# Zero-block products in TensorE's waits, earlier clearing of the dense sums and 96-row rotations in a two-block transformer kernel

## What is computed

```python
for l in range(2):                                  # first block
    h = rmsnorm(x, norm1_g[l]) * (1 + sc1) + sh1
    x = x + g1 * token_mix(h, ...)                  # w_in, recurrence, attention, w_out
    h = rmsnorm(x, norm2_g[l]) * (1 + sc2) + sh2
    x = x + g2 * grouped_moe(h, w_router, ...)      # top 2 of 16 experts
x = rmsnorm(x, final_g)
for layer in range(2):                              # second block
    y = recurrent_mixer(hn, ...) if layer == 0 else chunk_attention(hn, ...)
    h = h + g1 * y
    h = h + g2 * (square(relu(hn2 @ w1)) @ w2)      # dense MLP
```

## Time and profile before

| | us |
|---|---|
| median of 3 runs (2007.92 to 2010.44) | 2008.97 |
| the profiled execution | 2012.4 |
| its span | 2010.8 |
| PE busy in it | 1846.0 (92%) |

### The profile page before, as it was taken

One profiled execution on the slowest core, in us unless ns is written; L12 is line 12 of the kernel. 1 busy time (PEld: TensorE's weight loads), 2 busy tenths in 40 slices (PEclk: granted clock), 3 DMA queues, 4 the chain that ended last, 5 costly groups with the idle time before them and its releaser, 6 DMA issues.

```text
span 2010.8 us, 26693 instructions
## 1 busy us (share of the span) xinstructions
PE 1846.0 (92%) x11077; PEld 1309.6 (65%) x11080; DVE 675.8 (34%) x1189; ACT 591.5 (29%) x988; POOL 66.9 (3%) x136
## 2 busy tenths in 40 slices
PE   4999996989995999997999995999899999898998
PEld 2888685323333888684333334766699988588998
DVE  4583413000003583513000004313355551516554
ACT  2335311111113325311111112141254423525443
POOL 0000001100001000001101000000000000000000
PEclk8999997999997999997999997999899999998999
DMA  9669653999976665753999947879944553133540
GB/s 391 256 265 394 269 241 120 421 428 427 428 308 232 252 256 226 299 228 145 427 428 427 412 173 282 340 312 428 384 185 167 182 194 120 69 126 129 195 178 21
DMA packets 52732, 541.04 MB, mean 269 GB/s; under 512 B 6817, under 2 KB 11169, under 8 KB 21665
## 3 DMA queue, kind: packets, MB, share of 16 engines
q1 hardware_dynamic: 42656, 505.66, 62.4%
q0 software_dynamic: 9984, 34.09, 4.6%
HBM read 589.53 MB, written 29.62 MB: 308 GB/s over the span
## 4 chain that ended last, share of the span: by engine, by line
PE 82%; DMA 8%; DVE 6%; ACT 2%; DVEq 1%; issue 1%; SPq 0%; POOL 0%; POOLq 0%; ACTq 0%; PEldq 0%
PE bank L933 15%; PE bank L1230 14%; PE bank L896 9%; PE bank L897 9%; PE bank L898 9%; PE bank L1254 6%; DMA ring<-in_w_up 5%; PE bank L943 3%; PE bank L1060 1%; PE bank L1338 1%; PE bank L1426 1%; DMA ring<-in_ada 1%; PE bank L1359 1%; DMA ring<-in_lru_w_out 1%; PE bank L1208 1%
## 5 line engine op out<-in xcount | busy, mean ns | idle before, releaser
L896 PE MATMUL bank<-split_x,split_w 128*128 128x256 f32 x1024 | 292.3, 285 | 1.1 <-DVE split_w L2401 1.1
L897 PE MATMUL bank<-split_x,split_w 128*128 128x256 f32 x1024 | 291.9, 285 | 0.0
L898 PE MATMUL bank<-split_x,split_w 128*128 128x256 f32 x1024 | 291.8, 285 | 0.0
L896 PEld LDWEIGHTS bank<-split_x,split_w 128*128 128x128 f32 x1024 | 198.9, 194 | 2.9 <-DVE split_w L2401 2.9
L897 PEld LDWEIGHTS bank<-split_x,split_w 128*128 128x128 f32 x1024 | 198.9, 194 | 0.0
L898 PEld LDWEIGHTS bank<-split_x,split_w 128*128 128x128 f32 x1024 | 198.8, 194 | 0.0
L2283 DVE TENSOR_TENSOR hidden<-cqkv,bank 128x256 f32<-128x256 f32 x46 | 19.4, 421 | 523.7 <-ACT cqkv L1681 523.7
L2401 DVE TENSOR_TENSOR split_w<-ring,split_w 128x1024 fp32r<-128x1024 f32 x128 | 156.3, 1225 | 94.7 <-ACT split_w L1794 94.7
L933 PE MATMUL bank<-h_t,ring 128*128 128x256 f32 x736 | 164.5, 385 | 11.9 <-DVE h_t L2084 8.1
L933 PEld LDWEIGHTS bank<-h_t,ring 128*128 128x128 f32 x736 | 141.2, 193 | 35.9 <-DVE h_t L2084 9.3
L1794 ACT ACTIVATE split_w<-ring 128x1024 fp32r<-128x1024 f32 x128 | 133.8, 1049 | 94.4 <-PE bank L898 91.4
(11 more groups left out here) (351 smaller groups left out, 2322.9 us busy)
## 6 DMA issues: line engine op xcount, KB each, us to landing
ring<-in_ada SPq DMA_DIRECT2D x48, 2048.0 KB, 12.2
ring<-in_w_down SPq DMA_DIRECT2D x32, 2048.0 KB, 16.6
ring<-in_w_gate SPq DMA_DIRECT2D x32, 2048.0 KB, 13.1
ring<-in_w_up SPq DMA_DIRECT2D x32, 2048.0 KB, 18.3
ring<-in_mlp_w SPq DMA_DIRECT2D x32, 2048.0 KB, 7.7
ring<-in_w_in SPq DMA_DIRECT2D x16, 2048.0 KB, 11.9
mix<-in_w_gate SPq DMA_DIRECT2D x14, 2048.0 KB, 15.6
mix<-in_w_up SPq DMA_DIRECT2D x14, 2048.0 KB, 20.1
```

Of the source, the lines that this page charges most:

```text
L896: pe.matmul(out, hi, x_hi, start=start, stop=False, **kw)
L897: pe.matmul(out, hi, x_lo, start=False, stop=False, **kw)
L898: return pe.matmul(out, lo, x_hi, start=False, stop=stop, **kw)
```

## The change

A new helper issues `n` products of the zero block into a bank that nobody reads at that time:

```diff
+        def keep_busy(pe, bank, n):
+
+            for _ in range(n):
+                pe.matmul(bank[:, :], zeros[:, 0:P], zeros[:, :], start=True, stop=True, skip_group_check=True)
```

It is called ahead of waits of PE. In the first block, for each of two layers:

```diff
+                keep_busy(pe, banks[4], 36 if l else 42)
                 for name in ("f0", "f1", "q0", "q1"):
                     split_tiles(name)
...
-                turn = const("turn")[NOPE:DQK, :]
+                turn = const("turn")
...
-                    pe.matmul(b[0:DQK, :], turn, q_a[NOPE:DQK, 2 * i:2 * i + 2, :], start=True, stop=True)\
+                    pe.matmul(b[0:DQK, :], turn[0:DQK, :], q_a[0:DQK, 2 * i:2 * i + 2, :], start=True, stop=True)\
...
-                pe.matmul(b[0:DQK, 0:T], turn, krs[NOPE:DQK, :], start=True, stop=True)\
+                pe.matmul(b[0:DQK, 0:T], turn[NOPE:DQK, :], krs[NOPE:DQK, :], start=True, stop=True)\
...
+                keep_busy(pe, banks[7], 15)
                 pe.wait_ge(DV.sem, DV.at("h2 0", l))
                 b = job("router")
...
+                            keep_busy(pe, banks[7], 5)
                             pe.wait_ge(DV.sem, DV.at("h2 1", l))
...
+                keep_busy(pe, banks[7], 13)
                 pe.wait_ge(DV.sem, DV.at("picked", l))
...
+                    keep_busy(pe, banks[7], 21)
                     pe.wait_ge(AC.sem, AC.at("rows3", l))
                     pe.wait_ge(DV.sem, DV.at("one hot", l))
...
                 first_pair()
+                keep_busy(pe, banks[7], 4)
...
                 for t in range(TT):
+                    keep_busy(pe, banks[6], 4 if t else 47)
                     pe.wait_ge(MV.sem, MV.at(f"y{t}", l))
...
                     if k % 2 == 0:
+                        keep_busy(pe, banks[6], 2)
                         pe.wait_ge(AC.sem, AC.at(SQ0[k // 2], l))
```

In the second block:

```diff
+            keep_busy(pe, banks[6], 19)
             sum_squares(r_job("norm1"), h_t, KT, AR, SQ1).then_inc(PR.sem, PR.one("norm1"))
+            keep_busy(pe, banks[6], 15)
             pe.wait_ge(VR.sem, VR.at("h1 0"))
...
                     unit(R_AT[6], R_BASE)
                     unit(R_AT[7], R_BASE)
+                    keep_busy(pe, r_job("ri0"), 10)
...
-                pe.wait_ge(h2.sem, h2.at("h lo1"))
-                pe.drain().then_inc(pe_steps.sem, pe_steps.first)
-                clear_sums(pe)
+                pe.drain().then_inc(pe_steps.sem, pe_steps.first)
+                keep_busy(pe, banks[4 if layer else 7], 14)
+                pe.wait_ge(h2.sem, h2.at(H2[0]))
+                clear_sums(pe)
+                keep_busy(pe, banks[4 if layer else 7], 20)
+                pe.wait_ge(h2.sem, h2.at("h lo1"))
...
             sum_squares(a_job("norm"), h_t, KT, AA, SQ0).then_inc(PA.sem, PA.one("norm"))
+            keep_busy(pe, banks[7], 15)
             pe.wait_ge(VA.sem, VA.at("h 0"))
```

In `values_pe`, each of the six groups of the `"A "` half gets four such products in the group's own bank, and its wait moves behind them:

```diff
     for g in range(6):
-        pe.wait_ge(DV.sem, DV.at(f"{tag}p{g}", l))
         b = job(f"{tag}pT{g}")
+        for _ in range(4 if tag == "A " else 0):
+            pe.matmul(b[:, :], zeros[:, 0:P], zeros[:, :], start=True, stop=True)
+        pe.wait_ge(DV.sem, DV.at(f"{tag}p{g}", l))
```

More of the change, by code:

```diff
@@ L232, in scores_pe, with values_pe @@
         ins.then_inc(PE.sem, PE.one(f"{tag}s{g}"))
-def values_pe(pe, job, PE, AC, DV, l, tag, v, p, pT, ident):
+def values_pe(pe, job, PE, AC, DV, l, tag, v, p, pT, ident, zeros):
     for g in range(6):
+        b = job(f"{tag}pT{g}")
+        for _ in range(4 if tag == "A " else 0):
+            pe.matmul(b[:, :], zeros[:, 0:P], zeros[:, :], start=True, stop=True)
         pe.wait_ge(DV.sem, DV.at(f"{tag}p{g}", l))
-        b = job(f"{tag}pT{g}")
         for j in range(4):
@@ L1143, in _ @@
                 values_pe(pe, job, PE, AC, DV, l, "", lambda h, t: v_a[:, t, VD * h:VD * h + VD],
-                          p_a, pT_a, ident)
+                          p_a, pT_a, ident, zeros)
                 pe.wait_ge(AC.sem, AC.at("ov3", l))
@@ L1447, in _ @@
                           lambda h, t: v2_[:, t, HD * (8 * half + h):HD * (8 * half + h) + HD],
-                          p2_[half], pT2, ident)
+                          p2_[half], pT2, ident, zeros)
             pe.wait_ge(AA.sem, AA.at("B ov3"))
```

## The result

The changed kernel took **1991.66 us** (median of 4 runs, 1990.02 to 1992.88) beside 2008.93 for the kernel before in the same session: ratio 0.9911, 95% interval 0.9896 to 0.9927. Timed once more with two other kernels it took 1989.41 us beside 2010.28, ratio 0.9895 (0.987 to 0.992). It is faster, by 17 to 21 us. The prediction was 1980.7 with a range of 1974 to 1998: the sign and the range held, the sum of 28.3 us was too large.

The account below looks back on a forecast made before the run. The prediction took PE's work at the low clock, 108.05 us in 17 dips where stages change, as the recoverable cost. Its terms summed to -28.3 us, from the 2009.0 median to 1980.7, with a range of 1974 to 1998.

Parts of the forecast that it names:

- the first rival: Whole kernel: zero products don't hold the clock and fills run low at 0.43 us each; +36.5, 2045 us; 15%.
- the starts of the layers: Waits where each layer starts: fills fit, -0.2 us in all; under zeros that don't count, +6.6.
- Rotations: Layer 0 rotations widened to 96 rows: clock holds there and through the 48 conditioning products behind, -3.3 us.
- MLPs: Start of both MLPs: earlier drain -1.0 and full clock -2.4 in each, -6.8 us for both.
- both norms: Norm of the LRU: 16 products at full clock, -1.8 us; attention norm: rest of the dip halves, -1.85 us.
- half A: Attention probabilities, half A: four zero products per wait, sixth group and value products at full clock, -2.2 us.
- Router: Router in both layers: narrow products, counts and first pair gain from the full clock, -5.4 and -5.2, -10.6 us.
- the second rival: Router's narrow products drop the clock anyway; its 10.6 mostly lost, 1991 us, up to 1997 with the gate; 20%.
- The DMA-bound stretch keeps its length: Mixture: loads wait for PE's last use, so removing an earlier dip moves them too; 0 us change in the mixture.
- dips that move to other places in the mixture: Third rival: dips move within the mixture or LRU transfers take the shift back; half the sum, 1995 us; 5%.
- End of the mixture: Waits for y0, y1 and the sum of squares, where two zero products per pair set the end; -2.0 us both layers.
- Gate: First gate product in the LRU: ten uncovered products +2.15, dip perhaps prevented 1.7; +0.45 us, between +2.2 and 0.

Follow-up runs that it names:

- The two experiments on rows: Kernel before with rotations over 96 rows alone: 2007.25 us; changed kernel with its zero-product fills over 32 rows instead of 128: 2061.47 us.
- router unfilled: Changed kernel without the zero products around the router in each layer: 1995.22 us, ratio 0.9934 to the kernel before.
- the fills at blocks 6 to 8: Changed kernel plus zero products ahead of weight waits, blocks 6 to 8 of layer 0 and block 6 of layer 1: 1989.96 us, ratio 0.9898 to before.
- rotations alone: Kernel before with the 96-row rotations and nothing else: 2007.25 us, ratio 0.9981 to the kernel before.
- router interleaved: Changed kernel plus one zero product ahead of every second narrow product in the router's second tile, four per layer: 1989.29 us, ratio 0.9899 to before.
- mixture filled: Changed kernel plus zero products at mixture blocks 12, 14, 16 (layer 0) and 12 (layer 1), miscounted, mostly without waits: 2001.42 us, ratio 0.9966 to before.
- squares out: Changed kernel without zero products among the squares, the ten gate products ahead of the matrix waits: 1983.46 us, ratio 0.9880 to the kernel before.
- half fills: Changed kernel with half as many zero products in every fill: 1996.07 us, ratio 0.9924 to the kernel before.

## Why the prediction was right, and where its sum was off

- **Do zeros hold the clock?** Yes: the first rival (15%, 2045 us) is out. (Its own counts give 7.1 us for the starts of the layers, where I wrote 6.6; at 36.5 in all this has no weight.) My argument for zeros was that shape counts, not time, taken from the rotations. The two experiments on rows confirm it from both sides: 96 rows hold where 32 let go (in layer 0; in layer 1, 32 rows held once and let go once), and fills of 32 rows lose what fills of 128 keep.
- **Rotations, MLPs, both norms, half A.** Together 15.95 us were predicted (3.3 + 6.8 + 1.8 + 1.85 + 2.2), and the table gives 15.88. Each of these terms was worked out from rows at either clock level, and each came out within 0.15. The split of the MLP's 3.4 into 1.0 for the drain and 2.4 for the clock stands in the trace as 0.90 and 2.35.
- **Router: mechanism right, size 1.5 us too large.** I took the 24 narrow products at 2.9 us. They took 4.06 in layer 0, since the clock fell 1.4 us into them although fills stood on both sides, and 3.26 in layer 1, where it fell 2.2 us in. These 1.5 us are the whole miss of the term. On the dip itself the second rival was right. It was wrong that this costs nearly all of the 10.6: 9.1 came at the place, because the counts and the first pair behind the dip ran at the full clock. The median of 1991.66 is close to this rival's 1991, but not by its mechanism: 2.6 us of the router's 9.1 came back behind the second router ("router unfilled"), for another reason (next point).
- **"The DMA-bound stretch keeps its length": the step that failed.** In layer 0 it held (+0.26) through other dips at other places, and the fills at blocks 6 to 8 show why: dips ahead of the last wait are free. In layer 1 the stretch has only one wait, so anything at it counts. It grew by 1.48 and a dip of 1.7 came behind it. I gave this mechanism, dips that move to other places in the mixture, 5% and half of the sum; it occurred at a price of 3.2. The rotations alone already show the first half of it: PE 3.5 us sooner, the wait 1.05 longer. That a dip follows is not certain, and the length of the wait does not decide it: waits of 2.92 (both traces of the changed kernel) and 3.03 (router interleaved) had one, waits of 3.04 (mixture filled), 2.75 (squares out), 2.49 (rotations alone) and 2.06 (router unfilled) had none. Why the wait grew from 1.44 is not settled either: PE arriving 8.5 us later (router unfilled) took only 0.86 off it, 5.7 us later (half fills) all of it.
- **End of the mixture.** I had said that the two zero products set the pace and that 1.5 us more were to be had in each layer. Taking them out gave 1.3 to 1.4 in each.
- **Gate.** +0.45 predicted, from 2.15 for the ten products and 1.7 for the dip they prevent. Both were there; its matrix came 0.9 us sooner in relation to PE (a wait of 1.79 for 2.69), which made it -0.51. Ahead of the wait the same ten cost nothing, which gave the 1.84. That they are what prevents the dip rests on the one trace before: in "mixture filled" the clock fell in spite of them.

Of the 11.0 us between 28.3 and the 17.3 of the medians, 4.7 are the terms above. The other 6.3 are the choice of executions, 3.5 and 1.6 us of where the two profiled ones stand to their medians, and 1.2 of launch that the spans leave out. I had worked the sum out against a trace and then taken it from the median; with the 23.5 of the traces as the sum, the forecast would have been 1985.4, still 4 to 6 us below what was measured.

## What to carry to other kernels

Fill a wait of TensorE with zero products over all 128 rows, ahead of the wait that is last to end, to within some 0.4 to 1.4 us of its length as here: covered they are free and save what the work behind would lose at the 0.50 clock (0.6 to 2.4 us at each stage here, over 4 at a router, nothing at the starts of the layers, where DVE set the pace); not covered they cost 0.215 us each, so none belongs behind a transfer's wait or between work that PE itself paces. Real work over few rows is to be widened with zero rows where that is free. Before counting such a gain, ask whether a wait for transfers stands between the place and the end: a dip ahead of a stage's last such wait was worth nothing here, one behind it all of its 1.7 us.

## What the runs showed of the hardware

- TensorE at 0.50 while busy for 47.80 of 47.80 us, with zero products over 32 rows and 128-row work mixed; it fell 5.3 us into the first of them. Fewer rows fed, not idle time, lowered the clock; all-zero data over 128 rows held it.
- Eight products of 512 columns take 3.60 us over 96 rows, 3.67 over 32: rows cost no time, only the clock.
- The same router instructions kept the clock in one layer (308 to 315 us) and lost it in the other (906.5 to 916.7), and layer 0's dips in the mixture stood at 401 and 432 us or at 417 and 434, by kernel. Edits far away move such dips, at some 1.7 us each, which is why parts of this size were read at their place in a trace and not from the whole time.
